# Layer-norm sums folded on VectorE, a router on residual rows and a top-k on three partition groups in a trunk-layer kernel

## The chip, the cores and the metric

The kernel runs on one core of a Trainium2 chip, in float32. The metric is the time of one execution in device microseconds; lower is better. Three runs of the kernel before are given by their median and their extremes; one further execution was taken with the hardware profiler, and its trace is what the rows below come from.

## The reference, cut to what matters

One layer of a diffusion backbone is applied to 128 prompt rows and 512 sample rows of 1024 channels, each set with its own modulation and its own routing. The two parts that the change touches are the layer norm of the convolution branch and the expert-choice mixture of experts:

```python
def layernorm(x, g, b):
    mu = jnp.mean(xf, axis=-1, keepdims=True)
    var = jnp.mean(jnp.square(xf - mu), axis=-1, keepdims=True)
    y = (xf - mu) * lax.rsqrt(var + EPS)
...
v = rmsnorm(x, norm2_g) * (1 + sc2) + sh2
affin = jax.nn.softmax((v @ w_router).astype(jnp.float32), axis=-1)
g, idx = lax.top_k(jnp.swapaxes(affin, 1, 2), cap)
xe = jax.vmap(lambda xb, ib: xb[ib])(v, idx)
hdn = silu(xe @ w_e1) * (xe @ w_e3)
ye = (hdn @ w_e2) * g[..., None]
```

There are 16 experts; each takes its top 64 of the sample rows and its top 16 of the prompt rows, 80 rows (`CAP`), and the weighted results are added back to the rows. A final RMSNorm follows.

## The kernel before, in words

One function, `trunk_layer`, holds a program for each engine, and semaphores order them; within an engine the order is that of the code. Rows go in 5 tiles of 128 (`NT`), tile 0 the prompt; channels go in 8 blocks of 128 (`KD`). Products in float32 are made of three products of rounded parts (`hi`, `lo`): ScalarE rounds a weight to `hi`, VectorE takes the rest as `lo`, TensorE multiplies. A weight of 1024 x 512 comes in four pieces of 512 KB (`load_piece`, `piece_high` L690, `piece_low` L1024, `products` L1482), through four buffers; SyncE loads piece q when piece q - 4 is used up. Ten such groups follow the convolution and the recurrences: gates (0, 1, 4, 6), merges (2, 3, 5, 7) and the two halves of the output projection (8, at L1555, and 9, in `last_products` L1564).

**Layer norm** (L1158 to L1174 on VectorE, `squares` L772 on ScalarE). The channels lie on partitions, so the sums over channels are matmuls with a matrix of ones. L1519 multiplies the eight blocks of `cu` by it ahead of group 2; VectorE takes the mean off (`centre`); ScalarE squares each block into one of two buffers, `ln_sq`; L1542 multiplies two squared blocks by ones behind each piece of group 2.

**Router** (from L1219 on VectorE, L840 on ScalarE, L1564 on TensorE). `last_products(t)` makes the second half of row tile t, and `residual` adds both halves to the rows `xr`. ScalarE squares the row tile, takes the root and writes normalised rows `xn2` (`norm_rows`), which its DMA queue stores to `xn_dram` (the table that the experts gather from), beside the residual rows to `acc_dram`. `turn_normed(t)` transposes the eight blocks, VectorE and ScalarE scale and shift four each (`modulate_half`), and `router(t)` multiplies them by the router weights, with the 16 experts as the stationary operand. The 16 x 640 logits are turned back, the softmax is taken row tile by row tile (L1259 to L1267), and turned again.

**Top-k** (L1269 to L1285). On 16 partitions, eight rounds over 512 sample columns and two over 128 prompt columns; a round finds the eight largest, their places, and strikes them out. Two transpositions give 80 x 16 indices and gates.

**First expert.** GpSimd copies a column of indices (`gather` L599) and gathers 80 rows by an indirect DMA; TensorE turns them, VectorE modulates them (`modulate_xe`), ScalarE and VectorE split them, and the expert loop (L1640 on TensorE) begins. Its weights come in chunks of 2 MB through six ring slots; SyncE asks for chunks 0 and 1 behind the last product, 2 and 3 behind the last router, 4 and 5 behind the stores of the rows (L512 to L521). `hi_piece` (L875) rounds a chunk on ScalarE, `split_piece` (L1302) takes the rest on VectorE.

## Time and profile before

| what | value |
|---|---|
| runs, median of 3 | 1800.69 us (1800.22 to 1802.33) |
| profiled execution, own time | 1802.36 us |
| its span, first to last instruction | 1800.6 us |
| mean granted TensorE clock | 0.966 of full |
| TensorE busy in the span | 1669.5 us, 93% |
| VectorE / ScalarE / GpSimd busy | 1399.4 / 1101.8 / 275.3 us |
| TensorE busy in 632 to 685 us | 14.69 us of 53 |
| TensorE busy in 685 to 1795 us | 1091.35 us of 1110 |

The span is what the profiler sees; the own time has what lies around it too. A busy share is a mean over stages with different limits, so the chain of work that ended last and the timelines say more than the shares: the first two thirds of a millisecond are the dense layer, the rest is sixteen experts of equal length.

### The profile page before, as it was taken

The numbers are of one execution on the slowest core, as the hardware profiler recorded it, in microseconds if no ns is written. First come the engines' busy times: TensorE is split into PE (matmuls) and PEld (weight loads), VectorE is DVE, ScalarE is ACT, GpSimd is POOL, SyncE is SP. The second block draws the span as 40 slices with busy tenths as digits, with TensorE's granted clock in tenths as the row PEclk, the third lists the DMA queues.
The fourth block names the chain that finished last, engine by engine and source line by source line (L and its number), as shares of the span: only waits on it lengthen the run. The fifth ranks groups of instructions, "written<-read, shape, count | busy, mean of one in ns | idle before, by whom it ended". The sixth has DMA issues, their size and how long they took to land.

```text
span 1800.6 us, 21011 instructions
## 1 busy us (share of the span) xinstructions
PE 1669.5 (93%) x7966; PEld 1176.8 (65%) x7966; DVE 1399.4 (78%) x1308; ACT 1101.8 (61%) x859; POOL 275.3 (15%) x119
## 2 busy tenths in 40 slices
PE   4698889999999938999999999999999999999994
PEld 0298779778888725666666666666666666666662
DVE  0429999974334567988989989989989989989985
ACT  3325544542522335777777777777777777777773
POOL 2003435510000000002011012022022022022020
PEclk8799999999999968999999999999999999999997
DMA  9821111121325286999999999999999999999983
GB/s 389 312 67 57 39 61 40 50 68 59 96 71 165 104 338 237 362 391 366 378 390 373 376 390 359 389 386 367 386 389 362 383 387 371 381 390 370 379 337 124
DMA packets 142558, 492.49 MB, mean 274 GB/s; under 512 B 11257, under 2 KB 23705, under 8 KB 139456
## 3 DMA queue, kind: packets, MB, share of 16 engines
q1 hardware_dynamic: 137280, 475.75, 70.2%
q0 software_dynamic: 3776, 11.09, 2.8%
q10 hardware_dynamic: 1472, 5.25, 0.8%
q8 instruction: 18, 0.29, 0.1%
q14 instruction: 12, 0.10, 0.0%
HBM read 478.91 MB, written 13.16 MB: 273 GB/s over the span
## 4 chain that ended last, share of the span: by engine, by line
PE 81%; DVE 11%; DMA 5%; issue 1%; ACT 1%; SPq 0%; POOL 0%; DVEq 0%; another core or an unknown queue 0%; ACTq 0%; POOLq 0%
PE ps L1649 59%; PE ps L1493 12%; DVE ring L1076 5%; DMA ring<-in_w_mod 3%; PE ps L1455 2%; PE ps L1555 2%; PE ps L1573 1%; DVE ring L1104 1%; PE ps L1633 1%; DVE a_lo L1010 1%; PE ps L1390 1%; PE ps L1470 1%; DVE ring L1051 1%; PE ps L1627 1%; PE ps L1542 0%
## 5 line engine op out<-in xcount | busy, mean ns | idle before, releaser
L1307 DVE TENSOR_TENSOR ring_lo<-ring,w_hi 128x2048 fp32r<-128x2048 f32 x384 | 872.2, 2289 | 109.6 <-ACT w_hi L880 109.6
L880 ACT ACTIVATE w_hi<-ring 128x2048 fp32r<-128x2048 f32 x384 | 734.9, 1919 | 260.5 <-PE ps L1649 260.4
L1649 PE MATMUL ps<-w_hi,xe_hi 128*80 128x512 f32 x1024 | 402.9, 393 | 3.6 <-DVE xe_lo L1313 3.6
L1649 PE MATMUL ps<-ring_lo,xe_hi 128*80 128x512 f32 x1024 | 402.6, 393 | 0.0
L1649 PE MATMUL ps<-w_hi,xe_lo 128*80 128x512 f32 x1024 | 400.7, 391 | 0.0
L1649 PEld LDWEIGHTS ps<-w_hi,xe_hi 128*80 128x80 f32 x1024 | 151.8, 148 | 87.9 <-issue 4.3
L1649 PEld LDWEIGHTS ps<-w_hi,xe_lo 128*80 128x80 f32 x1024 | 151.7, 148 | 84.2 <-issue 0.5
L618 POOL DMA_INDIRECT acc_dram<-ya,idx_s x16 | 75.3, 4709 | 849.3 <-remote 849.3
L1649 PEld LDWEIGHTS ps<-ring_lo,xe_hi 128*80 128x80 f32 x1024 | 151.7, 148 | 81.0 <-issue 0.5
L1649 PE MATMUL ps<-w_hi,h_hi 128*80 128x512 f32 x512 | 203.1, 397 | 0.0
L1649 PE MATMUL ps<-ring_lo,h_hi 128*80 128x512 f32 x512 | 201.2, 393 | 0.0
L1649 PE MATMUL ps<-w_hi,h_lo 128*80 128x512 f32 x512 | 201.1, 393 | 0.0
L1455 PE MATMUL ps<-u_hi,a_hi 128*128 128x320 f32 x384 | 121.0, 315 | 7.7 <-ACT ring L735 4.1
L1076 DVE SCALAR_TENSOR_TENSOR ring<-ring,cur 128x113 f32<-128x113 f32 (+21 forms) x352 | 122.0, 425 | 0.0
L1455 PE MATMUL ps<-u_hi,a_lo 128*128 128x320 f32 x384 | 120.4, 314 | 0.0
L1455 PE MATMUL ps<-u_lo,a_hi 128*128 128x320 f32 x384 | 120.2, 313 | 0.0
L1026 DVE TENSOR_TENSOR b_lo<-ring,b_hi 128x1024 fp32r<-128x1024 f32 x40 | 49.8, 1256 | 84.1 <-ACT b_hi L697 83.8
L1649 PEld LDWEIGHTS ps<-w_hi,h_lo 128*80 128x80 f32 x512 | 75.8, 148 | 43.7
L697 ACT ACTIVATE b_hi<-ring 128x1024 fp32r<-128x1024 f32 x40 | 41.6, 1055 | 99.8 <-DMA ring<-in_w_in 53.1
L1649 PEld LDWEIGHTS ps<-w_hi,h_hi 128*80 128x80 f32 x512 | 75.7, 148 | 41.0
L1649 PEld LDWEIGHTS ps<-ring_lo,h_hi 128*80 128x80 f32 x512 | 75.7, 148 | 40.8
L594 POOL TENSOR_TENSOR ring<-ring 128x644 f32<-128x644 f32 x16 | 70.4, 4426 | 110.8 <-ACT ring L735 110.8
(234 smaller groups left out, 2048.6 us busy)
## 6 DMA issues: line engine op xcount, KB each, us to landing
ring<-in_w_e SPq DMA_DIRECT2D x192, 2048.0 KB, 10.1
ring<-in_w_mod SPq DMA_DIRECT2D x24, 1024.0 KB, 15.7
ring<-in_w_in SPq DMA_DIRECT2D x12, 1024.0 KB, 5.1
ring<-in_w_in SPq DMA_DIRECT2D x16, 512.0 KB, 3.6
xr<-in_x_sample SPq DMA_DIRECT2D x8, 512.0 KB, 5.8
ring<-in_w_rnn_out SPq DMA_DIRECT2D x8, 512.0 KB, 3.7
ring<-in_w_conv_out SPq DMA_DIRECT2D x8, 512.0 KB, 3.8
ring<-in_w_out SPq DMA_DIRECT2D x8, 512.0 KB, 4.1
```

What stands on the lines that cost most here:

```text
L594: eng.tensor_tensor(lr_i[:, t, d, :], lr_i[:, t, d, :], xc[:, t, :], ALU.mult).then_inc(ix_ready, 1)
L618: eng.indirect_dma_start(out=acc_dram, out_offset=bass.IndirectOffsetOnAxis(ap=idx_s[:, 0:1], axis=0), in_=ye, in_offset=None, compute_op= ...
L697: eng.activation(b_hi[q % 4][:, :, :], b_raw[:, q % 4, :, :], ACT.Copy).then_inc(piece_hi, 1)
L880: eng.activation(w_hi[m % 2][:, 2 * half:2 * half + 2, :], chunk(m)[:, 2 * half:2 * half + 2, :], ACT.Copy).then_inc(unit_hi, 1)
L1010: eng.tensor_tensor(a_lo[:, kind, :, :], wa(kind), a_hi[kind % 2][:, :, :].bitcast(F32), ALU.subtract)\
L1026: eng.tensor_tensor(b_lo[:, q % 4, :, :], b_raw[:, q % 4, :, :], b_hi[q % 4][:, :, :].bitcast(F32), ALU.subtract)\
L1076: ins = eng.scalar_tensor_tensor(out=cv[:, t, lo:hi], in0=glu[:, t, lo + s:hi + s], scalar=cur[:, G_CDW + k, t:t + 1], in1=cv[:, t, lo:hi] ...
L1307: eng.tensor_tensor(w_lo(m)[:, 2 * half:2 * half + 2, :], w, w_hi[m % 2][:, 2 * half:2 * half + 2, :].bitcast(F32), ALU.subtract)\
L1455: ins = eng.matmul(ps[:, b + h, 0:HALF], w[:, k, :], x[:, k, HALF * h:HALF * h + HALF], start=k == 0 and part == 0, stop=k == KD - 1 and p ...
L1493: ins = eng.matmul(ps[:, tile_bank(NT * g + t), :], x[:, k, P * t:P * t + P], w, start=k == 0 and n == 0, stop=k == KD - 1 and n == 2)
L1555: ins = eng.matmul(ps[:, tile_bank(NT * 8 + t), :], x[:, k, P * t:P * t + P], w, start=k == 0 and n == 0, stop=k == KD - 1 and n == 2)
L1649: ins = eng.matmul(ps[0:CAP, bank + b, :], x[:, k0 + kk, :], w[:, kk, 512 * b:512 * b + 512], start=first and kk == 0 and n == 0, stop=las ...
```

## The change

It has five parts.

- The layer norm's sums: VectorE adds the eight blocks up by halves (`fold_channels`: 2560, 1280, 640 columns), and TensorE multiplies the one block that is left by ones, once behind the first piece of group 2 and once behind its fourth. ScalarE squares all eight blocks into one area without waiting for a buffer.
- The router: the residual rows themselves are transposed, by halves of four blocks (`turn_early` when the first half of a row tile is done, `turn_late`), copied by ScalarE and VectorE (`copy_early`, `copy_late`), and multiplied by router weights that carry the scale (`wrs`), with the rows as the stationary operand and 16 columns streamed. The shift is multiplied by the router weights once (L1745 of the changed kernel); `logits` applies the row's root and adds the shift, giving logits with rows on partitions. These steps stand in the middle of the last products.
- The softmax is taken over all row tiles in one set of steps.
- The top-k: sample rows 0 to 255, sample rows 256 to 511 and prompt rows lie on three groups of partitions (from 0, 32, 64); eight rounds over 256 columns serve all. The second group's list is reversed, and of each pair of entries the larger is kept.
- The first gather reads the index table without a copy; chunks 4 and 5 are asked for behind it (`xe_loaded`); its rows are turned, modulated and split by halves. GpSimd clears the groups' areas behind the recurrences. In the expert loop the second half of the first product has a wait of its own.

```diff
             eng.wait_ge(logit_done, NT)
             load_chunk(0, 2)
             load_chunk(0, 3)
-            eng.wait_ge(vt_turned, NT)
             eng.wait_ge(rows_stored, 16 * 2 * NT)
+            eng.wait_ge(xe_loaded, 16)
             load_chunk(0, 4)
             load_chunk(0, 5)
...
             eng.wait_ge(rows_stored, 16 * 2 * NT)
-            gather(0)
+            eng.indirect_dma_start(out=xe, out_offset=None, in_=xn_dram,
+                                   in_offset=bass.IndirectOffsetOnAxis(ap=idx_t[:, 0:1], axis=0)).then_inc(xe_loaded, 16)
             step.restart()
             with eng.Fori(0, E) as i:
-                eng.wait_ge(xe_turned, i + 1)
+                eng.wait_ge(xe_turned, i + 2)
...
-                    if k >= 2:
-                        eng.wait_ge(ln_sq_used, k - 1)
-                    eng.activation(ln_sq[:, k % 2, :], cu[:, k, :], ACT.Square).then_inc(ln_squared, 1)
+                    eng.activation(ln_fold[:, N * k:N * k + N], cu[:, k, :], ACT.Square).then_inc(ln_squared, 1)
...
-            norm_rows(NT - 1)
-            modulate_half(NT - 1)
-            for t in range(NT):
-                eng.wait_ge(max_ready, 1)
-                eng.activation(soft[:, t, :], ps[:, 5, 16 * t:16 * t + 16], ACT.Exp, bias=sstat[:, 0, t:t + 1],
-                               accum_out=sstat[:, 1, t:t + 1]).then_inc(exp_ready, 1)
+                copy_early(t)
+            copy_early(NT - 1)
+            norm_root(NT - 1)
+            eng.wait_ge(max_ready, 1)
+            eng.activation(soft[:, :, :], soft[:, :, :], ACT.Exp).then_inc(exp_ready, 1)
+            norm_rows(4)
+            eng.wait_ge(groups_cleared, 6)
+            eng.wait_ge(best_ready, 1)
+            eng.activation(packed[0:E, 1, 0:CAP_S], best[0:E, :], ACT.Copy).then_inc(top_ready, 1)
+            eng.activation(packed[R_LATE:R_LATE + E, 1, 0:CAP_S][:, ::-1], best[R_LATE:R_LATE + E, :], ACT.Copy).then_inc(top_ready, 1)
+            eng.activation(packed[R_PROMPT:R_PROMPT + E, 1, CAP_S:CAP], best[R_PROMPT:R_PROMPT + E, 0:CAP_P], ACT.Copy)\
+                .then_inc(top_ready, 1)
...
             for m in range(2):
                 hi_piece(0, m, None)
-            hi_xe(1)
+            for h in range(2):
+                eng.wait_ge(xe_modulated, h + 1)
+                eng.activation(xe_hi[:, 4 * h:4 * h + 4, :], xeT[:, 4 * h:4 * h + 4, :], ACT.Copy).then_inc(xe_hi_ready, 1)
...
+            def fold_channels(rows):
+                half = KD * N // 2
+                step.did(eng.tensor_tensor(ln_fold[:, 0:half], rows[:, 0:half], rows[:, half:2 * half], ALU.add))
+                step.wait()
+                step.did(eng.tensor_tensor(ln_fold[:, 0:half // 2], ln_fold[:, 0:half // 2], ln_fold[:, half // 2:half], ALU.add))
+                step.wait()
+                eng.tensor_tensor(ln_fold[:, 0:N], ln_fold[:, 0:N], ln_fold[:, N:2 * N], ALU.add).then_inc(ln_folded, 1)
+            fold_channels(cu_f)
+            piece_low(10)
             eng.wait_ge(ln_summed, 1)
             step.did(eng.tensor_scalar(ln_mu.rearrange("p (h c) -> p h c", h=2), ps[:, 5:7, 0:HALF], -1.0 / D, None, ALU.mult))
             step.wait()
             centre(0, 4)
-            piece_low(10)
+            piece_low(11)
             centre(4, 8)
-            for q in range(11, 14):
-                piece_low(q)
-            eng.wait_ge(ln_sq_used, KD)
+            piece_low(12)
+            piece_low(13)
+            eng.wait_ge(ln_squared, KD)
+            fold_channels(ln_fold)
+            eng.wait_ge(ln_sq_summed, 1)
             eng.tensor_scalar(ln_rs.rearrange("p (h c) -> p h c", h=2), ps[:, 5:7, 0:HALF], 1.0 / D, EPS, ALU.mult, ALU.add)\
                 .then_inc(ln_var, 1)
...
+                    eng.wait_ge(wr_loaded, 16)
+                    for s in range(2):
+                        eng.tensor_tensor(wrs[:, :, s, :], wr[:, :, :], a2[:, :, s:s + 1].broadcast_to([P, KD, E]), ALU.mult)\
+                            .then_inc(wrs_ready, 1)
...
+            def copy_late(t):
+                eng.wait_ge(late_turned, t + 1)
+                eng.tensor_copy(x2T[:, 4:KD, P * t:P * t + P], ps[:, 2 * (t % 2) + 1, :].rearrange("p (k c) -> p k c", k=4))\
+                    .then_inc(late_copied, 1)
...
+                eng.wait_ge(r2_ready, t + 1)
+                eng.scalar_tensor_tensor(out=soft[:, t, :], in0=ps[:, (4, 7)[t % 2], 0:E], scalar=rstat[:, 3, t:t + 1],
+                                         in1=logit_shift[:, min(t, 1), :], op0=ALU.mult, op1=ALU.add).then_inc(logit_read, 1)
...
+            eng.wait_ge(shift_summed, 1)
+            eng.tensor_copy(shift_rows[:, :], ps[0:2, 3, 0:E]).then_inc(shift_rows_ready, 1)
...
+            residual(1, 0)
+            mean_square(0)
+            row_scale(0)
+            residual(1, 1)
+            copy_late(0)
+            mean_square(1)
+            row_scale(1)
+            copy_late(1)
+            logits(0)
...
+            mean_square(4)
+            row_scale(4)
+            logits(4)
...
+            for r in range(CAP_S // 8):
+                eight = best[:, 8 * r:8 * r + 8]
+                ins = eng.max(eight, lg[:, :])
+                if r < CAP_S // 8 - 1:
+                    step.did(ins)
                     step.wait()
...
+                else:
+                    ins.then_inc(best_ready, 1)
+                    eng.wait_ge(best_ready, 1)
+                step.did(eng.max_index(idx[:, 8 * r:8 * r + 8], eight, lg[:, :]))
+                if r < CAP_S // 8 - 1:
+                    step.wait()
+                    step.did(eng.match_replace(lg[:, :], eight, lg[:, :], -1.0))
+                    step.wait()
...
+            step.did(eng.tensor_tensor(pick[:, 0, :], v_early, gate_t[0:CAP_S, :], ALU.is_ge))
+            step.did(eng.tensor_tensor(idx_f[:, :], i_early, pick[:, 1, :], ALU.subtract))
+            step.wait()
+            step.did(eng.tensor_tensor(idx_f[:, :], idx_f[:, :], pick[:, 0, :], ALU.mult))
+            step.wait()
+            eng.tensor_tensor(idx_t[0:CAP_S, 0:E], idx_f[:, :], pick[:, 1, :], ALU.add).then_inc(idx_ready, 1)
+            eng.wait_ge(idx_ready, 1)
+            step.did(eng.tensor_tensor(gate_t[0:CAP_S, :], v_early, gate_t[0:CAP_S, :], ALU.max))
+            eng.tensor_copy(gate_t[CAP_S:CAP, :], ps[CAP_S:CAP, 0, CAP + R_PROMPT:CAP + R_PROMPT + E]).then_inc(idx_ready, 1)
...
+            for h in range(2):
+                eng.wait_ge(xe_turned, h + 1)
+                step.did(eng.tensor_tensor(halves[h].rearrange("p k c -> p (k c)"), ps[:, h, 0:4 * CAP],
+                                           xe_scale[:, 4 * h:4 * h + 4, :].rearrange("p k c -> p (k c)"), ALU.mult))
+            for h in range(2):
+                step.wait(1 - h)
+                eng.tensor_tensor(halves[h], halves[h], xe_shift[:, 4 * h:4 * h + 4, :], ALU.add).then_inc(xe_modulated, 1)
+            for h in range(2):
+                eng.wait_ge(xe_hi_ready, h + 1)
+                eng.tensor_tensor(xe_lo[:, 4 * h:4 * h + 4, :], halves[h], xe_hi[:, 4 * h:4 * h + 4, :].bitcast(F32), ALU.subtract)\
+                    .then_inc(xeT_ready, 1)
             step.restart()
-            split_xe(1)
...
+            def ones_times_fold(n, done):
+                eng.wait_ge(ln_folded, n)
+                for h in range(2):
+                    ins = eng.matmul(ps[:, 5 + h, 0:HALF], ones[:, :], ln_fold[:, HALF * h:HALF * h + HALF], start=True, stop=True)
+                ins.then_inc(done, 1)
...
+                    if g == 2 and p == 0:
+                        ones_times_fold(1, ln_summed)
+                    if g == 2 and p == 3:
+                        ones_times_fold(2, ln_sq_summed)
...
+                for k in range(4 * half, 4 * half + 4):
+                    ins = eng.matmul(ps[:, (4, 7)[t % 2], 0:E], x2T[:, k, P * t:P * t + P], wrs[:, k, min(t, 1), :],
+                                     start=k == 0, stop=k == KD - 1)
+                if half:
+                    ins.then_inc(logit_done, 1)
...
+                    if t >= 2 and k == 3:
+                        turn_early(t - 1)
+                        turn_late(t - 1)
+                        router(t - 2, 0)
+                        router(t - 2, 1)
+                        if t == NT - 1:
+                            turn_early(t)
                 ins.then_inc(tile_done, 1)
...
+            for k in range(KD):
+                ins = eng.matmul(ps[0:2, 3, 0:E], modc[:, 24 + k, :], wr[:, k, :], start=k == 0, stop=k == KD - 1)
+            ins.then_inc(shift_summed, 1)
+            last_products(0)
+            eng.wait_ge(shift_rows_ready, 3)
+            for s in range(2):
+                ins = eng.matmul(ps[:, 3, E * s:E * s + E], pick_row[:, s, :], shift_rows[:, :], start=True, stop=True)
+            ins.then_inc(shift_done, 1)
+            last_products(1)
+            eng.wait_ge(x2_ready, NT)
+            turn_early(0)
+            turn_late(0)
+            for t in range(2, NT):
                 last_products(t)
...
+            router(3, 0)
+            router(3, 1)
+            turn_late(4)
+            router(4, 0)
+            router(4, 1)
...
+            for k in range(KD):
+                ins = eng.transpose(ps[:, k // 4, CAP * (k % 4):CAP * (k % 4) + CAP], xe[:, P * k:P * k + P], ident[0:CAP, 0:CAP])
+                if k % 4 == 3:
+                    ins.then_inc(xe_turned, 1)
...
+                        if m == 0 and part:
+                            eng.wait_ge(xeT_ready, i * 2 + 2)
```

In VectorE's layer norm the rows stand, before (`cu` the branch, `gw` the mean's place, `ps` the sums), behind the copy of the last states:

```order
L1156 COPY last_t<-ps 16x128 [waits last_turned]
L1159 TENSOR_SCALAR gw<-ps 128x640 [waits ln_summed]
L1124 TENSOR_TENSOR cu<-cu,gw 128x640 [waits dve_step]
L1124 TENSOR_TENSOR cu<-cu,gw 128x640 x3
L1026 TENSOR_TENSOR b_lo<-ring,b_hi_62 128x1024 [waits piece_hi]
L1124 TENSOR_TENSOR cu<-cu,gw 128x640 x4
L1026 TENSOR_TENSOR b_lo<-ring,b_hi_63 128x1024 [waits piece_hi]
L1026 TENSOR_TENSOR b_lo<-ring,b_hi_60 128x1024 [waits piece_hi]
L1026 TENSOR_TENSOR b_lo<-ring,b_hi_61 128x1024 [waits piece_hi]
L1167 TENSOR_SCALAR ring<-ps 128x640 [waits ln_sq_used]
```

and now:

```order
L1196 COPY last_t<-ps 16x128 [waits last_turned]
L1201 TENSOR_TENSOR ring<-cu 128x2560
L1203 TENSOR_TENSOR ring<-ring 128x1280 [waits dve_step]
L1205 TENSOR_TENSOR ring<-ring 128x640 [waits dve_step]
L1066 TENSOR_TENSOR b_lo<-ring,b_hi_62 128x1024 [waits piece_hi]
L1210 TENSOR_SCALAR gw<-ps 128x640 [waits ln_summed]
L1164 TENSOR_TENSOR cu<-cu,gw 128x640 [waits dve_step]
...
L1066 TENSOR_TENSOR b_lo<-ring,b_hi_63 128x1024 [waits piece_hi]
L1164 TENSOR_TENSOR cu<-cu,gw 128x640 x4
L1066 TENSOR_TENSOR b_lo<-ring,b_hi_60 128x1024 [waits piece_hi]
L1066 TENSOR_TENSOR b_lo<-ring,b_hi_61 128x1024 [waits piece_hi]
L1201 TENSOR_TENSOR ring<-ring 128x2560 [waits ln_squared]
```

Three adds stand ahead of piece 10 and three behind piece 13; the first ones wait for nothing but the engine itself, the second ones for all squares.

On TensorE, in tile 4 of the last products and behind it, stood before (`ring` holds `xn2` in L1583 and the modulated rows in L1593):

```order
L1573 MATMUL ps<-b_hi_60,m_hi 128x512 [waits x2_ready]
...
L1583 MATMUL ps<-ident,ring 128x128 [waits vt_act,vt_dve,xn2_ready]
L1583 MATMUL ps<-ident,ring 128x128 x7
L1593 MATMUL ps<-ring,wr 16x128 [waits lg_ready,vt_act,vt_dve]
L1593 MATMUL ps<-ring,wr 16x128 x7
L1583 MATMUL ps<-ident,ring 128x128 [waits vt_act,vt_dve,xn2_ready]
...
L1593 MATMUL ps<-ring,wr 16x128 [waits lg_ready,vt_act,vt_dve]
...
L1583 MATMUL ps<-ident,ring 128x128 [waits vt_act,vt_dve,xn2_ready]
...
L1593 MATMUL ps<-ring,wr 16x128 [waits lg_ready,vt_act,vt_dve]
...
L1593 MATMUL ps<-ring,wr 16x128 [waits lg_ready,vt_act,vt_dve]
...
L1614 MATMUL ps<-ident,lg 128x16 [waits lg_ready] x5
```

and now (`xr` the residual rows, `ring` their transposed copy):

```order
L1730 MATMUL ps<-b_hi_60,m_hi 128x512 [waits x2_ready]
...
L1693 MATMUL ps<-ident,xr 128x128 [waits early_copied,x2_ready]
...
L1704 MATMUL ps<-ident,xr 128x128 [waits late_copied,x2_ready]
...
L1716 MATMUL ps<-wrs,ring 128x16 [waits logit_read,early_copied]
...
L1716 MATMUL ps<-wrs,ring 128x16 [waits late_copied]
...
L1693 MATMUL ps<-ident,xr 128x128 [waits early_copied,x2_ready]
...
L1730 MATMUL ps<-b_hi_62,m_hi 128x512
...
L1716 MATMUL ps<-wrs,ring 128x16 [waits logit_read,early_copied]
...
L1716 MATMUL ps<-wrs,ring 128x16 [waits late_copied]
...
L1704 MATMUL ps<-ident,xr 128x128 [waits late_copied,x2_ready]
...
L1716 MATMUL ps<-wrs,ring 128x16 [waits logit_read,early_copied]
...
L1767 MATMUL ps<-ident,gw 80x128 [waits soft_ready]
```

A transposition and a router for earlier tiles, and half of tile 4's own transposition, have moved ahead of the second half of the tile's products; behind them stand two routers and half a transposition.

On ScalarE, behind the last root, stood before:

```order
L847 ACTIVATE rstat<-rstat 128x1 [waits ms2_ready]
L849 ACTIVATE ring<-xr,rstat 128x1024 [waits r2_ready]
L851 DMA xn_dram<-ring 128x1024 [waits xn2_ready]
L852 DMA acc_dram<-xr 128x1024
L858 ACTIVATE ring<-ps,modc,a 128x128 [waits vt_turned]
...
L871 ACT_TABLE_LOAD
L871 ACTIVATE soft,sstat<-ps,sstat 128x16 [waits max_ready] x5
L880 ACTIVATE w_hi_68<-ring 128x2048 [waits w_loaded0,rows_stored,logit_done]
...
L880 ACTIVATE w_hi_69<-ring 128x2048 [waits w_loaded1]
...
L885 ACTIVATE xe_hi<-ya 128x640 [waits xe_modulated]
```

and now:

```order
L878 ACTIVATE rstat<-rstat 128x1 [waits ms2_ready]
L903 ACT_TABLE_LOAD
L903 ACTIVATE soft<-soft 128x80 [waits max_ready]
L882 ACTIVATE ring<-xr,rstat 128x1024 [waits r2_ready]
L883 DMA acc_dram<-xr 128x1024
L885 DMA xn_dram<-ring 128x1024 [waits xn2_ready]
L907 ACTIVATE gw<-best 16x64 [waits best_ready,groups_cleared]
L908 ACTIVATE gw<-best 16x64
...
L918 ACTIVATE w_hi_68<-ring 128x2048 [waits w_loaded0,rows_stored,logit_done]
...
L918 ACTIVATE w_hi_69<-ring 128x2048 [waits w_loaded1]
...
L956 ACTIVATE xe_hi<-ya 128x320 [waits xe_modulated] x2
```

The row stores of the last tile stand behind the exponential, and the rounding of the first two chunks (`w_hi`) behind the copies of the best values.

## Rows read from the trace of the kernel before

**Rows 1.** Chain that ended last, in order of time: start us, us, what.

```profile
385.30 8.62 PE ps L1519 x32
393.91 6.85 PE ps L1493 x30
400.76 2.15 PE ps L1542 x8
...
603.02 1.24 DVE b_lo L1026
604.30 12.54 PE ps L1573 x54
616.84 0.87 PE ps L1583 x8
...
674.16 5.68 DMA ya<-xn_dram,idx_g
...
684.86 35.12 PE ps L1649 x144
```

**Rows 2.** Timeline of VectorE, layer norm: start, busy us, engine, line, operation [idle before].

```profile
376.53 5.56 DVE L1151 TENSOR_TENSOR ya_lo<-ya,y_hi 128x2560 fp32r<-128x2560 f32 x2 [1.12 <-ACT y_hi L793]
...
394.81 3.03 DVE L1124 TENSOR_TENSOR cu<-cu,gw 128x640 f32<-128x640 f32 x4
...
405.54 1.23 DVE L1026 TENSOR_TENSOR b_lo<-ring,b_hi 128x1024 fp32r<-128x1024 f32 x1 [2.49 <-ACT b_hi L697]
```

**Rows 3.** Timeline of ScalarE, layer norm, columns as above.

```profile
395.67 1.47 ACT L777 ACTIVATE ln_sq<-cu 128x640 f32<-128x640 f32 x2 [8.90 <-DVE cu L1124]
...
404.45 1.06 ACT L697 ACTIVATE b_hi<-ring 128x1024 fp32r<-128x1024 f32 x1 [0.70 <-DMA ring<-in_w_rnn_out]
```

**Rows 4.** Timeline of VectorE, softmax, top-k and the first split.

```profile
649.11 0.19 DVE L1264 RECIPROCAL sstat<-sstat 128x5 f32<-128x5 f32 x1 [1.46 <-ACT soft L871]
...
651.40 0.68 DVE L1276 MAX8 gates_e<-lg 16x8 f32<-16x512 f32 x1
...
653.68 0.68 DVE L1276 MAX8 gates_e<-lg 16x8 f32<-16x512 f32 x1
...
668.75 0.26 DVE L1276 MAX8 gates_e<-lg 16x8 f32<-16x128 f32 x1
...
669.81 0.28 DVE L1276 MAX8 gates_e<-lg 16x8 f32<-16x128 f32 x1
...
671.53 4.49 DVE L1307 TENSOR_TENSOR ring_lo<-ring,w_hi 128x2048 fp32r<-128x2048 f32 x2
```

**Rows 5.** Weight loads of TensorE, 596 to 690 us, by form: busy us, mean ns.

```profile
L1593 PEld LDWEIGHTS ps<-ring,wr 128*16 128x16 f32 x80 | 8.0, 105 | 3.0 <-issue 1.6
L1573 PEld LDWEIGHTS ps<-b_hi,m_lo 128*128 128x128 f32 x40 | 7.5, 188 | 1.6
...
L1583 PEld LDWEIGHTS ps<-ident,ring 128*128 128x128 f32 x40 | 4.5, 140 | 3.5 <-ACT ring L849 2.9 <-issue 0.2
```

**Rows 6.** Timeline of GpSimd, first gather.

```profile
671.56 2.31 POOL L601 COPY idx_g<-idx_t 80x1 uint32<-80x1 uint32 x1 [306.01 <-DVE gate_t L1289]
674.16 2.73 POOL L603 DMA_INDIRECT ya<-xn_dram,idx_g  x1 [0.29 <-POOL idx_g L601]
```

**Rows 7.** Instructions of line L603: duration ns min/median/max.

```profile
L603 POOL DMA_INDIRECT ya<-xn_dram,idx_g x17: 936/2700/2734, 674.2 to 1724.7; - x17
```

**Rows 8.** Two windows: us, busy of PE, PEld, DVE, ACT, POOL; clock, DMA, GB/s.

```profile
624.00:632.00 8.00, 8.00 (x47) 6.59 (x47) 3.25 (x9) 4.01 (x8) 0.00 (x0) 1.00 0.41 163
640.00:648.00 8.00, 6.68 (x45) 4.71 (x43) 2.34 (x8) 3.10 (x8) 0.00 (x0) 0.79 1.06 406
```

**Rows 9.** Costliest groups, page: busy us, mean ns, idle before and its releaser.

```profile
L880 ACT ACTIVATE w_hi<-ring 128x2048 fp32r<-128x2048 f32 x384 | 734.9, 1919 | 260.5 <-PE ps L1649 260.4
```

**Rows 10.** DMA issues, page: count, KB each, median us to landing.

```profile
ring<-in_w_e SPq DMA_DIRECT2D x192, 2048.0 KB, 10.1
...
ring<-in_w_rnn_out SPq DMA_DIRECT2D x8, 512.0 KB, 3.7
```

271 lines of the change are left out of this document (143 added, 128 removed).

## The prediction

> **What bounds the kernel now.** I read the chain that ended last first, in order of time [rows 1]. The reader is to see that up to 604 us, and again from 684.86 us to the end, one piece of TensorE work follows the next, and that between them stand some fifty short pieces of VectorE, ScalarE, GpSimd and DMA work in which TensorE waits for the choice of tokens and the first gather. So a microsecond is worth its full price in three places: on TensorE in the layer norm (L1519, L1542), on TensorE among the last products (L1573 to L1593), and anywhere on the thin path from there to the first expert product. After that, 16 experts follow at TensorE's pace: ScalarE's rounding of the weights waits for TensorE 260.4 us and for nothing else [rows 9], so no DMA sets that pace. The change leaves the expert loop alone but for one wait more per expert; whatever is won before 684.86 us should reach the end.
>
> Then I read the timelines of VectorE [rows 2, 4], ScalarE [rows 3] and GpSimd [rows 6], which price the new steps and show who would hide them, the weight loads of TensorE [rows 5] for a router with its operands exchanged, and the granted clock [rows 8].
>
> The sum is made in the profiled execution: 1802.36 us by its own time, span 1800.6 us. The median of the runs is 1800.69 us, 1.67 us below; I take the difference off the median. About 0.2%, 3.6 us, is what a measurement of this kernel can tell from no change.
>
> **Layer norm.** Removed are 32 instructions of L1519, 8.62 us, and four groups of 8 of L1542 at 2.15 us [rows 1]: 17.2 us, all on the path. Added are 2 times 4 of the same instructions, 0.27 us each by L1519, 2.15 us. TensorE now also meets the copy of the last states at once (it must wait some 0.4 us for it; the sums hid that). That is -14.7 us, provided that VectorE's folds are done in time. A fold is three adds of 2560, 1280 and 640 columns: 2.8 us (half of L1151's 5.56), some 1.5 (between L1026's 1.23 for 1024 and that) and 0.8 (a quarter of L1124's 3.03) [rows 2], with two hops 5.2 us. The first begins when VectorE has copied the states, some 0.3 us behind 385.30, and ends at 390.9; TensorE, now in the first piece of the group for 6.85 us [rows 1], asks at 392.5. The second is tighter. TensorE comes to it after three further pieces, at 392.5 + 1.1 + 3 x 6.85 = 414.2 us. Before it VectorE must centre eight rows (6.1 us) and split three pieces, ScalarE must square eight rows (0.74 each) and round the pieces, and piece 13 lands only some 3.7 us [rows 10] after its buffer is free at 400.5; in the trace too ScalarE waits for such a landing [rows 3]. That puts ScalarE's last square at 406.7 and the fold at 406.8 to 411.9, 2.2 us before TensorE asks. I cost both folds at nothing; if that cover is gone each costs up to 5.2 us. The merge behind the second sum waits for it as it does now.
>
> **Last products.** TensorE waits for the fourth piece, whose split ends at 603.02 + 1.24 us [rows 1], until 604.30; that wait hides the new shift product of eight two-column matmuls. VectorE however must copy its result before the first residual, which I put 2 us later, so its split of that piece starts at about 603.5 instead of 603.02: +0.45 us. From there TensorE has 102 products left, at 12.54 us for 54 [rows 1] 23.7 us. Ahead of the last one now stand nine half-tile transpositions (0.87 us for 8 blocks [rows 1], so 0.44 each, 3.9 us), three routers and 0.3 us for spreading the shift. The old router loaded 16 columns and streamed 128; the new one loads 128 columns sixteen times and streams 16, so the load sets its time. No such form is in the trace. The bounds are the 105 ns load of L1593 and the 188 ns load of L1573; I take the 140 ns load of the transpositions, which are followed by equally short work [rows 5]: 16 x 0.14 = 2.24 us, bounds 1.7 and 3.0. The Trainium skill (TensorE: Matmul & The Clock Gate, LDWEIGHTS) says a load's time goes with its columns, over 1.2 GHz, an estimate of 107 ns here, and would speak against loading 128 instead of 16; by it the five routers would take 1.7 us each and the sum would be 2.6 us better than mine; the trace's 105 ns for 16 columns does not follow that rule.
> So the last product ends at 604.75 + 23.7 + 3.9 + 6.7 + 0.3 = 639.4 us; that is some 7 us later than now, and the first two chunks of the experts' weights are asked for that much later.
>
> **Router tail, softmax, top-k.** Behind the last product: router 3 (2.2), the late half of tile 4 turned, copied and multiplied (0.4 + 0.8 + 1.1), one read with scale and shift; 5.0 us. ScalarE's root for tile 4 runs beside this. The softmax is now seven small vector steps, one exponential and two transpositions. A step like L1264 takes 0.19 us [rows 4] and about 0.1 to be seen by the next: 3.2 us with the copy of 80 x 256. A top-k round of 512 columns takes 653.68 - 651.40 = 2.28 us, one of 128 takes 669.81 - 668.75 = 1.06 us [rows 4]; linear in the columns, 256 cost 1.47. Partitions run side by side there, so 80 cost what 16 cost. Eight rounds, the last without its replace, are 11.3 us, against about 19 now. The merge adds three index sums, two transpositions and eight short steps: 2.4 us. Index ready at 639.4 + 21.9 = 661.3 instead of 671.56: -10.3 us from 604.30 on.
>
> ScalarE rounds chunks 0 and 1 only behind its copies of the best values, where it now does so early. Four activations of 1.92 us [rows 9] are done by 666, while the gather flies, and the first split on VectorE by 666 too; they are hidden, with 1 to 2 us to spare.
>
> **First gather.** Now: index ready 671.56, GpSimd's copy 2.31 us, the indirect DMA on GpSimd 2.73 us, landing at 674.16 + 5.68 = 679.84 [rows 1, 6]: 8.3 us. The copy ends 0.1 us behind the first half of VectorE's split that began beside it [rows 4], and the indirect DMA takes from 0.94 to 2.73 us, median 2.70 [rows 7]: GpSimd waits for a vector instruction in flight. Without the copy the DMA itself meets the split's first half, 2.25 us, then needs 0.94, and lands 2.95 us later (679.84 - 676.89): 6.2 us, -2.1. With chunks 4 and 5 behind it, no weights compete with it; they didn't at 674 us either, so that part is worth nothing to the gather. They are then asked for at 667.5 and land in some 10 us [rows 10], at 678; ScalarE wants chunk 4 only three units of 5.5 us behind the first product, 686. Hidden.
>
> **Halves of the first rows.** From the landing to the first product now 684.86 - 679.84 = 5.0 us. By halves the vector and scalar steps of half width overlap; I count 3.4 us: -1.6.
>
> **Sum.** -14.7 - 10.3 - 2.1 - 1.6 = -28.7 us, so 1772.0 us. What I may have left out are hops between engines, more likely a loss.
>
> **Rivals.** (1) The folds don't free TensorE: the second, or both, comes late and TensorE waits instead. For: VectorE's margin is 2 us and hangs on a landing. Against: VectorE idles for much of these 50 us now. Price up to 2 x 5.2, typically 7 us: 1779. That is also the case in which the change does only half of what it says.
> (2) The clock. It is granted in full to 632 and falls while TensorE has little to do, 0.79 on the mean of 640 to 648 [rows 8]. The new routers put stretches of 2 to 3 us with hardly a column streamed between the last products. If it fell to 1.2 GHz at the first of them and stayed, 60 products would cost 0.23 us more each and the small work some 4: 1772 + 18 = 1790. Against: the present transpositions and routers stand there too, and the clock is full.
> (3) GpSimd's descriptors don't wait for VectorE. Then the gather is 0.94 + 2.95 = 3.9 us and the time 1769.7. The rows speak against it: 2.70 us in the median [rows 7]. The Trainium skill (SBUF — State Buffer, Who interferes with whom) infers that a two-input vector instruction does not hold up descriptors; by it 1769.7 would be the time.
> (4) Slower: the weight stream. The moved chunks and the earlier start could leave the experts' loads so far behind that DMA paces them. From 684.86 us to the end of the span an expert has 69.7 us (1115.7 by 16) for twelve chunks; two under way at a landing of 10.1 us [rows 10] take 60.6. It decides once the landing passes 11.6 us; at 12.4 an expert takes 74.4 and sixteen lose 75 us: 1847. Against: ScalarE never waits for weights now [rows 9], and a chunk's buffer is still freed six units ahead.
>
> **How the numbers follow.** Forecast 1772.0: chance 0.75, own range 1767 to 1778 (routers from -2.6 to +3.8 us, unlisted hops up to 2 us, gather to -2). Rival 1: 0.10, rival 2: 0.07, rival 3: 0.05, rival 4: 0.03. The range 1766 to 1782 takes in the forecast's bounds, rival 1 and rival 3 and leaves out rivals 2 and 4. Faster 0.95: all but rival 4 and a mix of mishaps; within 0.2%: 0.02; slower: 0.03.
>
> **What would show it.** Right: four matmuls over ones behind the first and the fourth piece of the first merge group, with no wait for VectorE before them; last product about 7 us later against the fourth piece's split; rounds of 1.5 us; GpSimd's first indirect DMA of some 3 us; the first expert product near 656 us; the same period per expert. Wrong: a wait on the second fold of over 2 us; routers of 3 us or more; a clock below 1 before the last product; ScalarE waiting for weights.

## The result, and the profile after

| | before | after | ratio, 95% interval |
|---|---|---|---|
| device time, median | 1801.24 us (4 runs, 1800.22 to 1802.33) | 1774.88 us (4 runs, 1772.81 to 1777.6) | 0.9855 [0.984, 0.987] |
| profiled execution, time and span | 1802.36, 1800.6 us | 1772.81, 1771.0 us | |

The change makes the kernel faster by 26.4 us on the medians; the prediction said 28.7 and 1772.0. The profiled executions show all of the 28.7, but of the kernel before it is an execution as slow as the slowest of its four, and of the changed one the fastest of its four. The rest of this text is about the difference, and about which steps came out for the reasons given.

The chain that ended last, after the change (start us, us, what), from the layer norm to the first expert product. Between the last router and the gather (627 to 645 us) it names the last tile's row store, which lands at 638.87; the index is ready at 645.62, so the top-k is what the gather waits for:

```profile
384.36 0.29 DVE last_t L1196
...
384.69 7.09 PE ps L1618 x30
391.79 1.08 PE ps L1646 x4
392.87 20.45 PE ps L1618 x90
413.32 1.09 PE ps L1646 x4
...
582.81 4.97 DMA ring<-in_w_out
...
588.89 1.24 DVE b_lo L1066
...
590.18 1.66 PE ps L1730 x6
591.84 0.54 PE ps L1750 x4
592.38 5.67 PE ps L1730 x24
...
623.79 1.69 PE ps L1716 x16
...
645.91 5.92 DMA ya<-xn_dram,idx_t
...
655.35 14.78 PE ps L1803 x54
```

The 32 and 4 x 8 products over ones [rows 1] have become two groups of 4, and the first expert product stands at 655.35 instead of 684.86 us. VectorE's second fold in its timeline (start, busy us, engine, line, operation, [idle before]):

```profile
405.85 2.83 DVE L1201 TENSOR_TENSOR ring<-ring 128x2560 f32<-128x2560 f32 x1
408.71 1.49 DVE L1203 TENSOR_TENSOR ring<-ring 128x1280 f32<-128x1280 f32 x1
410.24 0.82 DVE L1205 TENSOR_TENSOR ring<-ring 128x640 f32<-128x640 f32 x1
414.43 0.82 DVE L1220 TENSOR_SCALAR ring<-ps 128x640 f32<-128x640 f32 x1 [3.37 <-PE ps L1646]
```

The fold ends at 411.06, 2.3 us before TensorE asks for it at 413.32, and TensorE doesn't wait. The top-k round and the first gather, from the timeline:

```profile
631.04 0.42 DVE L1368 MAX8 best<-lg 80x8 f32<-80x256 f32 x1
...
632.54 0.42 DVE L1368 MAX8 best<-lg 80x8 f32<-80x256 f32 x1
...
645.65 4.49 DVE L1420 TENSOR_TENSOR ring_lo<-ring,w_hi 128x2048 fp32r<-128x2048 f32 x2
645.91 2.90 POOL L643 DMA_INDIRECT ya<-xn_dram,idx_t  x1 [279.82 <-remote]
651.96 1.30 PE L1790 MATMUL ps<-ident,ya 80*128 80x80 f32 x8 [8.09 <-DMA ya<-xn_dram,idx_t]
```

A round takes 1.50 us for 80 partitions and 256 columns, against 2.28 and 1.06 for 512 and 128 [rows 4]. And in the page's groups, where before the row of [rows 9] stood, ScalarE's waits in the expert loop:

```profile
L918 ACT ACTIVATE w_hi<-ring 128x2048 fp32r<-128x2048 f32 x384 | 734.9, 1918 | 260.1 <-PE ps L1803 259.9
```

From the first expert product to the end the span has 1115.65 us, and had 1115.74: the extra wait per expert costs nothing that shows.

### The profile page after: what moved, and what is told of

The parts are those of the page before. It is cut to its first block, busy times and chain, and to the rows that moved or that the text cites. A ratio compares the mean times of both kernels' runs of the same rounds, so it can differ in the third digit from the quotient of the medians.

```text
span 1771.0 us, 20907 instructions
## 1 busy us (share of the span) xinstructions
PE 1655.0 (93%) x7922; PEld 1168.0 (66%) x7922; DVE 1401.4 (79%) x1306; ACT 1096.5 (62%) x839; POOL 262.5 (15%) x124
## 4 chain that ended last, share of the span: by engine, by line
PE 82%; DVE 10%; DMA 5%; issue 1%; ACT 1%; another core or an unknown queue 0%; SPq 0%; DVEq 0%; POOLq 0%; ACTq 0%
PE ps L1803 60%; PE ps L1618 12%; DVE ring L1116 5%; DMA ring<-in_w_mod 3%; PE ps L1580 2%; PE ps L1678 2%; PE ps L1730 1%; DVE ring L1144 1%; PE ps L1783 1%; DVE a_lo L1050 1%; PE ps L1515 1%; PE ps L1595 1%; DVE ring L1091 1%; DMA xn_dram<-ring 1%; PE ps L1777 0%
## 5 line engine op out<-in xcount | busy, mean ns | idle before, releaser
L918 ACT ACTIVATE w_hi<-ring 128x2048 fp32r<-128x2048 f32 x384 | 734.9, 1918 | 260.1 <-PE ps L1803 259.9
```

The lines of the kernel that those rows point to most:

```text
L918: eng.activation(w_hi[m % 2][:, 2 * half:2 * half + 2, :], chunk(m)[:, 2 * half:2 * half + 2, :], ACT.Copy).then_inc(unit_hi, 1)
```

## The experiments

Twelve experiments in three groups, each with four or five runs (before_padded has eleven) beside the kernel before, whose median in the groups was 1800.83, 1801.5 and 1801.23 us. Times given are medians; "slower than the change" is against its second timing, 1775.5 us, so across groups a few tenths of a microsecond are the groups' own.

### The change once more (again)

No edit.

> The changed kernel itself, timed once more beside the three that follow; nothing is edited. Theory one (its four times, 1772.81 to 1777.6, differ by noise in every part alike): median 1774 to 1776, and from the end of the last product to the index 22.0 us, from the index to the first expert product 9.7 us, as in its first profile (623.7, 645.62, 655.35). Theory two (in some executions the last tile's row stores land after the index is ready and hold the first gather back): in a longer execution GpSimd's indirect DMA starts later than 0.3 us behind the index and the chain names the store there. The fourth weight piece took 5.0 us to land where before it took 3.67: if that was chance, it is back near 3.7 here and the piece's split some 1.3 us earlier in the same distance from its issue.

Measured: 1775.5 us (1772.4 to 1775.7). Its profile, of an execution of 1775.67 us, differs from the first in one place:

```profile
582.14 5.11 DMA ring<-in_w_out
...
589.64 1.90 PE ps L1730 x6
591.54 0.96 PE ps L1750 x4
592.50 8.15 PE ps L1730 x24
```

TensorE has waited 2.7 us for the fourth weight piece, as in the first profile (2.6; before the change it was 2.0); behind it 24 products take 8.15 us instead of 5.67. The first product behind the wait, in TensorE's timeline, before and in the first profile of the change:

```profile
604.30 0.50 PE L1573 MATMUL ps<-b_hi,m_hi 128*128 128x512 f32 x1 [1.99 <-DVE b_lo L1026]
```

```profile
590.18 0.50 PE L1730 MATMUL ps<-b_hi,m_hi 128*128 128x512 f32 x1 [2.61 <-DVE b_lo L1066]
```

The windows of this run (us; busy of PE, PEld, DVE, ACT, POOL; clock, DMA, GB/s) say why:

```profile
590.00:594.00 4.00, 4.00 (x14) 2.93 (x13) 3.56 (x7) 0.00 (x0) 0.00 (x0) 0.61 0.00 0
594.00:598.00 4.00, 4.00 (x12) 3.08 (x11) 0.50 (x3) 3.52 (x5) 0.00 (x0) 0.54 0.02 6
598.00:602.00 4.00, 4.00 (x23) 3.39 (x22) 1.27 (x2) 0.86 (x2) 0.00 (x0) 1.00 0.63 256
```

The granted clock falls behind the wait, to 1.2 GHz for most of 8 us, which costs 0.24 + 0.42 + 2.48 = 3.1 us. In the first profile it stays at 1.00:

```profile
590.00:594.00 4.00, 3.82 (x17) 2.99 (x18) 3.86 (x8) 0.00 (x0) 0.00 (x0) 1.00 0.00 0
```

So the difference between the two profiled executions has one place: neither theory on record, though theory one's numbers fit. The row stores are out: GpSimd's gather starts 0.29 us behind the index in both. And the load's 5 us were no chance.

### The layer norm alone put back (ln_on_pe)

```diff
-            fold_channels(cu_f)
...
-            fold_channels(ln_fold)
-            eng.wait_ge(ln_sq_summed, 1)
+            eng.wait_ge(ln_sq_summed, KD)
...
+                for k in range(KD):
+                    ins = eng.matmul(ps[:, 5 + h, 0:HALF], ones[:, :], cu[:, k, HALF * h:HALF * h + HALF],
+                                     start=k == 0, stop=k == KD - 1)
```

> The changed kernel with the layer norm alone put back on TensorE: 16 products with ones ahead of the third group, and 16 more in pairs behind the pieces, no folds on VectorE. Theory (the whole of the layer norm's gain is TensorE's own time, 17.2 us less the 2.15 that stay and a short wait): slower than the changed kernel by 14.0 to 15.0 us, 1789 to 1790; VectorE's variance step near 429 instead of 414.4. Rival (the folds beside the product stream slowed the splits, or gave time back later): slower by under 12 us.

Measured: 1785.71 us, 10.2 slower than the change: the rival's number. Of its two reasons the first is out, since no split is slower in the layer norm (1.22 to 1.23 us with the folds and without); the chain shows 8.62 us and groups of 2.15 back in their places, so TensorE's own time there is as predicted. The second holds: the time is given back 170 us later:

```profile
597.67 3.66 DMA ring<-in_w_out
...
603.72 1.67 PE ps L1729 x6
...
605.93 5.69 PE ps L1729 x24
```

Here the fourth piece loads in 3.66 us, TensorE waits 1.3 us and the clock stays. So the folds win 14.7 and about 4.5 of it is given back: by the two profiles (this one and that of the change once more) 1.4 by the longer load, 3.1 by the clock behind it.

### Why the load is longer (pe_padded, before_padded)

In the DMA answer of the changed kernel for 585 to 590 us one packet of the instruction queue moves while the load ends (queue, packets, MB, share):

```profile
q1 hardware_dynamic: 157, 0.29, 15.9%
q8 instruction: 1, 0.02, 1.2%
```

Before, that packet moved at 588 to 590, ahead of the load's start at 598. The pad adds TensorE instructions where TensorE waits anyhow; it went into both kernels.

```diff
-            for n in range(16, 24):
+            for n in range(16, 18):
                 mod_products(n)
+            for n in range(20):
+                eng.matmul(ps[:, 5, 0:16], ident[:, :], ident[:, 0:16], start=True, stop=True)
+            for n in range(18, 24):
+                mod_products(n)
```

> The changed kernel with 20 small TensorE products of ident (nobody reads them) in TensorE's long wait for the modulation weights near 66 us; all later work as it is. In the changed kernel the fourth piece's load took 5.0 to 5.15 us in five profiles, and a 0.02 MB packet of the instruction queue moves inside it (584 to 588); before and with the layer norm on TensorE the load took 3.65, and that packet moved 9 us ahead of it. Theory one (the packet is a fetch of TensorE's own instructions, which the change moved in time by taking instructions out; the piece's last descriptor waits behind it): the packet moves some 9 us earlier, the load takes 3.7, TensorE's wait there falls from 2.7 to 1.3, its clock stays at 1.00 behind it, and the time is 1770.5 to 1772.5, 1.5 to 4.3 below the changed kernel. Theory two (the load is long for another reason, or the fetch is another engine's): the load still takes 5.1 and the time is 1773 to 1776.

> The kernel before, with the same 20 small TensorE products in its wait for the modulation weights, whose results nobody reads. In the padded changed kernel TensorE's clock stood at 1.00 when the products that follow the modulation began (0.75 without them), and those ended 2.6 us earlier. Theory one (the pad does two things: 2 to 2.6 us early on by the clock, and some 3.5 to 4 at the fourth piece, where before had nothing to repair, since its load took 3.65 and its clock stayed at 1.00): before becomes 1798.3 to 1799.5, and the change is then worth 29 to 30 on the padded pair (1769.3). Theory two (the pad helps both alike): before becomes 1795 to 1796.

Measured: the changed kernel 1769.31 us (1769.12 to 1769.79), the kernel before 1799.61 (ratio 0.9991 [0.9982, 1.0]), a little above the range of theory one and far from theory two's. The padded change stands 1.2 below the range of its theory one, for the second effect told below. Its chain:

```profile
580.17 3.62 DMA ring<-in_w_out
...
586.18 1.66 PE ps L1734 x6
...
588.38 5.67 PE ps L1734 x24
```

The packet now moves at 574 to 576, the load takes 3.62, TensorE waits 1.3 us, the clock stays, and the spread of the five runs is 0.7 us. Over all profiles: in the six with the packet outside this load it takes 3.62 to 3.84 us, in the eight with the packet inside 4.97 to 5.15. The added instructions are TensorE's alone and moved the packet, so it is TensorE's instruction fetch, which the change had moved by taking instructions out.

Where in the load the packet falls matters. Between 350 and 600 us the fourteen traces have 263 loads of 512 KB with no other transfer and no instruction packet beside them: 3.47 to 4.18 us. Of 14 loads with one such packet (16384 bytes) beginning 2.3 to 2.96 us behind the load's issue, 13 take 4.85 to 5.15 (one 3.62). With that packet in the first 1.3 us a load takes 3.60 to 4.48, and with it at 2.98 us or later 3.51 to 4.05. In the padded change it falls 0.95 us into the third piece's load, which takes 4.08 and which TensorE doesn't wait for. In the change, 260 of the load's 272 packets have begun by 586 us, and the other 12 follow until 587.1; the load has landed at 587.78. That these 12 queue behind the instruction packet is argued only.

The Trainium skill (Runtime: NRT & Kernel Launch, Instruction fetch mechanics) has instructions fetched in blocks of 16 KiB at a cost that is mostly hidden; the packet's 16384 bytes agree, and here the cost isn't hidden but falls on another transfer.

The pad has a second effect that I had not meant. TensorE's clock is 1.00 instead of 0.75 in 86 to 94 us, and the first products behind the modulation end 2.6 us earlier. In the kernel before it is worth 1.6 us on the median. On the padded pair, where no fetch falls into the load, the change is worth 1799.61 - 1769.31 = 30.3 us.

### The wait covered by other products (tiles_paired)

```diff
-            last_products(0)
+            last_products(0, 0, 6)
...
-            last_products(1)
+            last_products(1, 0, 6)
+            last_products(0, 6)
+            last_products(1, 6)
```

> The changed kernel with one change of order on TensorE: the first six products in k of tiles 0 and 1 of the last group go before the two tiles' last two, which need the fourth piece. Theory one (TensorE's wait of 2.7 us for the fourth piece is on the path, and where its clock falls behind that wait, 24 products take 8.0 us instead of 5.6): the wait is covered by 4.1 us of tile 1's products, the clock stays at 1.00 from 583 to 618, and the time is 1769 to 1771.5, 3 to 6 below the changed kernel. Theory two (the wait only moves: VectorE's residual of the first tile comes 1.5 us later and TensorE waits for that, or the softmax waits elsewhere): within 1 us of the changed kernel, 1774 to 1776.

Measured: 1772.37 us (1769.52 to 1772.49), 3.1 less than the change but above theory one. In the profile, of the execution of 1769.52, the wait is gone and the clock stays; the chain then runs through VectorE's first residual and ScalarE's norm of the first tile, as theory two has it, though TensorE waits for them only 0.6 us in all. What the other four executions lost was not profiled and stays open.

### The top-k alone put back (topk_rows16)

Sixteen rows of 512 and then 128 columns as before, behind the new softmax; no copies of the best values on ScalarE.

> The changed kernel with the top-k put back to 16 rows of 512 and 128 columns, one after the other, no groups and no merge. Theory (as in the prediction): from the exponential's end to the index 21.9 us as before (649.58 to 671.55), where the groups take 15.8, so slower than the changed kernel by 5.5 to 6.5, 1780 to 1782; but the first four chunks have then landed long before the gather, which should come down faster than the 5.96 us of the changed kernel, so 2 us of that may come back: 1778 to 1780. Rival (the merge's small steps eat the rounds' gain): within 2 us of the changed kernel.

Measured: 1780.14 us, 4.6 slower. In the two chains the time from the softmax's first vector instruction to the gather's start is 654.77 - 630.23 = 24.5 us, against 18.05 in the change: 6.5, as expected. But the gather lands 5.92 us after its start here too, although the DMA engines are quiet by then (busy 0.01 and 0.00 in 654 to 656 and 656 to 658 us), so the 2 us that I expected to come back didn't come this way; the profiled executions, in both of which the clock fell behind the fourth piece, stand 6.2 us apart (1781.83 and 1775.67), the medians 4.6; the difference is within what the executions of the change spread.

### What the first gather waits for (split_late, chunk4_held, chunks_unheld)

Three edits. First, VectorE's split waits until GpSimd has written the gather's descriptors:

```diff
+            eng.memset(idx_off[0:R_LATE, :], float(NP)).then_inc(gather_asked, 1)
...
+            eng.wait_ge(gather_asked, 1)
             split_piece(0, 0)
```

> The changed kernel, but VectorE begins the split of the first expert's first weight piece only when GpSimd has issued the first gather (GpSimd clears one small tile behind the indirect DMA and signals). Theory one (GpSimd's descriptor writing waits while VectorE runs the split's 2.25 us halves, as 2.90 us here against 0.94 elsewhere): the indirect DMA takes about 0.95 us, the gather lands 1.9 us earlier, near 650, and the first product comes 1.0 to 1.6 us earlier, since the split then ends about 651.4. Theory two (its 2.90 us are its own or those of busy DMA queues): it stays near 2.9, the split begins about 649 and ends about 653.5, and the first product is 1 to 3 us later.

Second, that and the fourth chunk also behind the gather:

```diff
-            load_chunk(0, 3)
             eng.wait_ge(rows_stored, 16 * 2 * NT)
             eng.wait_ge(xe_loaded, 16)
+            load_chunk(0, 3)
```

> The changed kernel with the split behind the gather's descriptors, as in the run with the late split, and the fourth weight chunk also asked for only when the first gather has landed. In that run the indirect DMA fell from 2.90 to 1.00 us and the gather still landed 5.96 us after its start. Theory one (the gather's landing is set by the DMA engines, which still move the first four chunks until some 2.4 us before it): with 2 MB less ahead the gather lands 4.0 us after its start, the first product comes 1 to 2 us earlier (the split then ends about as late), and the time is 1.0 to 2.0 us below that of the late split. Theory two (5.9 us is what such a gather takes): it lands 5.9 after its start, and the time does not move, or rises if the fourth chunk then comes too late for its products.

Third, the change with its fifth and sixth chunk not held back (without the line `eng.wait_ge(xe_loaded, 16)`):

> The changed kernel with the fifth and sixth weight chunk asked for behind the row stores alone, as before, not behind the first gather. Theory (as in the prediction: holding them back is worth nothing, since the queue still moves the first four chunks then): within 0.5 us of the changed kernel, and the gather's landing near 5.9 us from its start. Rival (the two chunks take the DMA engines from the gather): the gather lands 1 to 3 us later and so does the first product.

Measured: 1773.66, 1773.83 and 1778.63 us. The indirect DMA and the first transposition behind it in the late split's timeline, with a window (DMA share and GB/s last), then the same of the held chunk, and the step in the chain of the unheld ones:

```profile
648.20 1.00 POOL L644 DMA_INDIRECT ya<-xn_dram,idx_t  x1 [283.09 <-remote]
654.30 1.30 PE L1793 MATMUL ps<-ident,ya 80*128 80x80 f32 x8 [8.14 <-DMA ya<-xn_dram,idx_t]
...
648.00:650.00 2.00, 0.00 (x0) 0.00 (x0) 0.45 (x1) 2.00 (x2) 1.12 (x2) 0.50 1.01 403
```

```profile
647.74 1.00 POOL L644 DMA_INDIRECT ya<-xn_dram,idx_t  x1 [281.21 <-remote]
651.72 1.30 PE L1793 MATMUL ps<-ident,ya 80*128 80x80 f32 x8 [6.03 <-DMA ya<-xn_dram,idx_t]
...
648.00:650.00 2.00, 0.00 (x0) 0.00 (x0) 0.91 (x1) 2.00 (x2) 0.86 (x2) 0.50 0.32 61
```

```profile
648.21 9.28 DMA ya<-xn_dram,idx_t
```

GpSimd's 2.90 us become 1.00 as soon as VectorE's split is out of the way: GpSimd does wait for it. Yet the gather lands as late as ever, 5.96 us after its start, since the DMA engines still move the first four chunks. Only with both gone does it land after 3.85 us. Each cause alone gives 5.9 and hides the other: in the run with the old top-k the engines were quiet and the descriptors took 2.90. With the split late and the fourth chunk held, the first product stands 8.6 us behind the index instead of 9.7: half of the 2.1 us is lost again, since VectorE is at the late split until 653.6 and modulates the rows only then. On the medians neither edit is worth more than the spread, and the 1.0 to 2.0 us expected between them did not come. Holding chunks five and six back, which I had called worth nothing, is worth 3.1 us: without it the gather lands 9.28 us after its start.

### Index copy and whole rows put back (gather_as_before)

```diff
-            eng.indirect_dma_start(out=xe, out_offset=None, in_=xn_dram,
-                                   in_offset=bass.IndirectOffsetOnAxis(ap=idx_t[:, 0:1], axis=0)).then_inc(xe_loaded, 16)
+            gather(0)
...
-            for h in range(2):
-                eng.wait_ge(xe_modulated, h + 1)
...
+            eng.wait_ge(xe_modulated, 2)
+            eng.activation(xe_hi[:, :, :], xeT[:, :, :], ACT.Copy).then_inc(xe_hi_ready, 2)
```

> The changed kernel with two parts put back: GpSimd copies the first index column ahead of the first gather, and the first expert's tokens are modulated, rounded and split whole instead of by halves. Theory (the prediction's terms): index to landing 8.3 us instead of 6.2, landing to first product 5.0 instead of 3.4, so 3.7 us slower than the changed kernel, 1778 to 1779.5. Rival (the copy is free, since the weight chunks hold the gather until about 4 us behind the index anyway): the gather's landing moves by less than 0.5 us, and the time rises by 1.6 alone.

Measured: 1777.76 us. In its chain (start us, us, what):

```profile
648.18 2.37 POOL idx_g L635
650.64 0.13 issue
650.77 5.64 DMA ya<-xn_dram,idx_g
...
661.60 35.23 PE ps L1796 x144
```

The gather lands 8.3 us behind the index (ready at 648.11), the first product follows 5.2 us later: 13.5 us, against 9.7 in the change. Both terms hold in the trace, 3.8 us together. The profiled execution took 1779.02, 3.4 more than the change's with the same fall of the clock; the medians show 2.3 of it. The copy is not free: it delays the gather past the chunks, and the descriptors still wait for VectorE.

### A version that beats both (first_gather, first_gather_warm)

The padded change, with the late split and the held chunk, the gather begun on the indices alone, and the first weight piece split by halves:

```diff
-            eng.wait_ge(idx_ready, 3)
+            eng.wait_ge(idx_ready, 1)
...
+            eng.wait_ge(gather_asked, 1)
+            split_piece(0, 0, (0,))
...
+            split_piece(0, 0, (1,))
             split_piece(0, 1)
...
-                    eng.wait_ge(unit_split, units(i, m))
+                    eng.wait_ge(unit_split, units(i, m, 0 if m == 0 else 1))
...
+                        if m == 0 and kk == 2:
+                            eng.wait_ge(unit_split, units(i, 0))
```

> The padded changed kernel (1769.3), with the stretch from the index to the first expert product made over: GpSimd begins the first gather on the expert indices alone (the gate values and the last column follow), the fourth weight chunk is asked for behind the gather, VectorE splits the first half of the first weight piece once the descriptors are written, and the second half behind the token halves, and TensorE waits for the two halves apart. Theory (port and queue each hold the gather at about 5.9 us and must both be taken away): the indirect DMA starts 0.6 us earlier, lands 3.9 us after its start, and the first product comes 2.0 to 3.0 us earlier: 1766.3 to 1767.5. Rival (the late fourth chunk or the late second half stops TensorE, or one more wait per expert costs time): 1768.5 or above, with TensorE waiting for VectorE's split or ScalarE for a weight chunk among the first expert's products.

Then the same with 11 products of `ident` behind the softmax's transpositions and 4 behind those of the index, 512 columns each:

> The run with the first gather made over, and 11 TensorE products of ident with 512 columns (nobody reads them) while VectorE picks the top eight, and 4 more while the gather is under way. In the changed kernel the clock is 0.50 from 632 to 656, the first 11 expert products come every 0.43 us instead of 0.23, and the transposes of the gathered rows take 1.30 us. Theory (the clock follows TensorE's own work): at 0.85 us each the added products fill 9.4 and 3.4 us, the clock is 1.00 at the first expert product, and 2.0 to 3.0 us come off the first gather's run. Rival (they run at half clock, 1.7 us each, and the index transposes or the gathered rows wait for them): slower than the first gather's run by 1 to 6 us.

Measured: 1766.82 us (ratio to before 0.9808 [0.9795, 0.9822]) and 1766.34 (0.9802 [0.9788, 0.9815]). The first is 2.5 us below the padded change, inside the expected range; its gather lands 4.06 us after its start. The second gains no more than the spread, though its clock is as the theory wanted, in the windows:

```profile
632.00:636.00 4.00, 4.00 (x11) 1.85 (x10) 3.73 (x14) 0.00 (x0) 0.00 (x0) 1.00 1.03 422
...
648.00:652.00 4.00, 1.80 (x8) 1.21 (x9) 3.86 (x7) 2.34 (x4) 1.37 (x3) 1.00 0.93 312
```

and the expert products come every 0.23 us from the first on. The chain tells where it went:

```profile
650.39 6.70 DVE ring_lo L1423 x3
...
657.13 27.79 PE ps L1818 x120
```

TensorE now waits for VectorE's splits of the first two pieces, until 657.13. Without the added products the first eight come every 0.43 us, and TensorE asks for the second piece at 657.46, just behind that split: the half clock there was all but covered by it. In the change itself it was not: TensorE asks for the second piece at 663.06 us, 3.0 behind the end of its split (660.02). Its first 24 products take 7.71 us there, against 5.58 with the added products, so half clock costs up to 2.1 us in the change, an estimate: no run took that part alone.

## Why the prediction was right, and where it was not

Counted from the end of the states' transposition (385.30 before, 384.34 after) to the first expert product, the profiled executions have 299.56 and 271.01 us: -28.55, where the sum said -28.7. The other 0.96 us of the -29.51 lie in work that the change doesn't touch. That the sum fits to 0.2 us is partly luck: the fourth piece came out 0.9 us worse than written and the last products 1.0 us better, and the two cancel. By steps:

| step | predicted | profiled | what differs |
|---|---|---|---|
| layer norm | -14.7 | -14.7 (17.24 out, 1.08 + 1.09 + 0.35 in) | the 30 products of the first piece, 7.09 instead of 6.85 us |
| to the fourth piece's split | +0.45, by VectorE | +1.3 | a load of 4.97 instead of 3.65 us; VectorE begins 0.02 us behind ScalarE |
| last products, from there | 34.65 | 33.6 (590.18 to 623.79) | three routers of 1.70 us instead of 2.24; the rest 0.6 more |
| last product to index | 21.9 | 21.8 (to 645.62) | routers less, the merge more |
| index to landing | 6.2 | 6.2 | right sum, half of the cause |
| landing to first product | 3.4 | 3.5 | nothing |

**The fourth piece.** The failed step is "+0.45 us": I let VectorE's copy of the shift delay the split and took the load's time over from before. The runs show the load 1.3 us longer, by a fetch of TensorE's instructions that the shorter layer norm had moved into it. No row of before could price this; the order of TensorE's instructions and the instruction queue's packets in the DMA answer could have warned of it.

**The clock.** Rival 2 had the mechanism in the wrong place and at the wrong size: not at the new routers, where the clock is 1.00 in every profile of the change, but behind the wait for the fourth piece, and for some 8 us, not for the rest: 3.1 us instead of 18. In three variants the clock does fall inside the router of the last tile, which then takes 2.07 (tiles_paired), 2.42 (first_gather_warm) and 2.68 us (first_gather) instead of 1.86; so rival 2's place is real too, at a price of 0.2 to 0.8 us. "The clock is full" held for the first profiled execution and for none of the next six profiles with the packet inside the load and the wait on the path; in one of these the fall costs only 1.3 us. It is the likeliest reason why the median is 2.9 us above the forecast, and for most of the 4.8 us by which the change's runs spread: without packet and wait the padded change spreads by 0.7. The executions without a profile can't show it. What decides in which executions the clock falls behind waits of 2.6 to 2.8 us stays open.

**Routers.** A router's 16 loads and products take 1.70 us in the trace of the change, one per 106 ns. My 140 ns, from transpositions, was not right, and it came from the wrong column. The view of [rows 5] shows of the new form (busy us, then mean ns of one):

```profile
L1716 PEld LDWEIGHTS ps<-wrs,ring 128*128 128x128 f32 x80 | 9.5, 192 | 0.2
```

A mean of 192 ns at a spacing of 106 ns means that the records of loads overlap, so that column gives no price for a load. The Trainium skill's rule for a load (TensorE: Matmul & The Clock Gate, LDWEIGHTS), an estimate of 107 ns for 128 columns, agrees with the spacing. What I held against it, 105 ns for 16 columns [rows 5], was a mean of the same column, in which the 128-column loads have 192: it does not speak against the rule. What set the pace of the old router was not tried. (By its own sum, 639.4 against 631.6, the prediction moved the last product 7.8 us, not "some 7"; measured from the fourth piece's split it is 33.6 us instead of 27.3.)

**First gather.** The wait of GpSimd for VectorE is real, so rival 3 falls: 2.90 against 1.00 us. The Trainium skill (SBUF — State Buffer, Who interferes with whom) infers that descriptors don't wait for such a two-input step; these runs decide against it for this indirect DMA, which also reads its indices from SBUF; which part of it waits they don't show. But the prediction's "no weights compete with it" failed: the first four chunks do, and alone would give the same 5.9 us, so the 6.2 us came out right with half of their cause. And "worth nothing to the gather", said of chunks five and six, failed by 3.1 us. I judged them by where the gather stood before, at 674 us; in the change it stands 28 us earlier, among them.

**Rivals 1 and 4.** The folds left TensorE no wait: the second was done 2.3 us before TensorE asked, where the prediction said 2.2. ScalarE waits for TensorE 259.9 of its 260.1 us in the loop, so DMA doesn't pace it.

## What to carry to other kernels

Price each transfer and each queue at the time at which it will stand after the change, not where it stands now: a step pulled forward meets other traffic, and two waits of like length can hide each other, so that removing either shows nothing. Where a load's wait is on the path, look also at what else moves on the DMA engines then, instruction fetches among it, and at the clock behind the wait; a wait 1.4 us longer cost 4.5 in the profiles in which the clock fell. And a stretch at half clock costs only what no other engine's work covers.
